# One hundred gathered tokens on one run of partitions, and two table units fetched early

## The reference

```python
def peer(h, w_pq, sub_keys, u_tab, v_tab):
    qr = (h @ w_pq)                                  # 8 heads, two halves of 128
    sc = einsum(qr, sub_keys)                        # 128 scores per half
    s_top, i_top = top_k(sc, 16)                     # 16 of each half
    c_top, c_pos = top_k(all 256 sums of pairs, 16)  # 16 of the 256 pairs
    expert = i0 * 128 + i1                           # 16384 experts
    g = softmax(c_top)
    a = gelu(einsum(u_tab[expert], h), approximate=False)
    return einsum(g * a, v_tab[expert])
x = x + peer(rmsnorm(x, g_ffn), ...)
```

## Time and profile before

| what | value |
|---|---|
| time, median of three runs | 1666.11 us |
| profiled execution, its own time | 1668.66 us |
| its span, first to last instruction | 1666.9 us |
| mean granted TensorE clock | 0.998 |
| busy PE / DVE / ACT / POOL | 1654.3 / 1019.7 / 503.4 / 273.2 us |
| moved by DMA | 569.90 MB |
| first matmul of the u stage at | 511.99 us |
| first matmul of the v stage at | 1101.08 us |

### The profile page before, as it was taken

The page is one execution under the profiler, slowest core; times in us unless marked ns, Lnnn a source line. Parts: engine busy times, 40 slices in busy tenths (PEclk is TensorE's granted clock), DMA queues, the critical chain, the costliest instruction groups (busy, mean ns, idle before and its releaser), DMA issues.

```text
span 1666.9 us, 28850 instructions
## 1 busy us (share of the span) xinstructions
PE 1654.3 (99%) x11438; PEld 1569.3 (94%) x11438; DVE 1019.7 (61%) x1709; ACT 503.4 (30%) x1347; POOL 273.2 (16%) x252
## 2 busy tenths in 40 slices
PE   8999999999999999999999999999999999999999
PEld 6768888888999999999999999999999999999998
DVE  5426695767878999767777767753334333443333
ACT  6547567756551000035444454410000000000000
POOL 1020000000003222312222122121121212211110
PEclk9999999999999999999999999999999999999999
DMA  9764446466648999999999999999999999999996
GB/s 342 240 143 132 140 129 200 139 226 204 227 153 342 421 396 423 417 380 419 404 422 413 422 409 422 422 422 421 421 421 417 417 415 422 422 421 420 421 416 234
DMA packets 107057, 569.90 MB, mean 342 GB/s; under 512 B 11281, under 2 KB 13457, under 8 KB 48209
## 3 DMA queue, kind: packets, MB, share of 16 engines
q1 hardware_dynamic: 56768, 216.22, 35.0%
q0 software_dynamic: 31792, 220.50, 32.7%
q10 hardware_dynamic: 18432, 132.41, 19.3%
HBM read 563.04 MB, written 4.46 MB: 340 GB/s over the span
## 4 chain that ended last, share of the span: by engine, by line
PE 82%; DMA 12%; DVE 3%; issue 1%; ACT 1%; POOL 0%; ACTq 0%; DVEq 0%
PE ps L1586 33%; PE ps L1531 22%; PE ps L1318 5%; PE ps L1323 5%; PE ps L1320 5%; DMA acts<-in_u_rows,sel 5%; DMA late<-in_u_rows,sel 3%; DMA sel<-sel 2%; PE ps L1340 2%; PE ps L1482 2%; PE ps L1478 2%; PE ps L1477 2%; DVE w_lo L821 1%; DMA raw<-in_w_in 1%; PE ps L1548 1%
## 5 line engine op out<-in xcount | busy, mean ns | idle before, releaser
L1145 DVE SCALAR_TENSOR_TENSOR acts<-late,sel,acts 128x2048 f32<-128x2048 f32 x77 | 181.1, 2352 | 247.3 <-DMA late<-in_v_tab,sel 247.0
L1531 PE MATMUL ps<-acts,late 128*128 128x160 f32 x2048 | 287.9, 300 | 0.0
L1531 PE MATMUL ps<-acts,raw 128*128 128x160 f32 x2048 | 287.6, 300 | 0.0
L1586 PE MATMUL ps<-acts,raw 128*128 (+1 forms) x2048 | 283.8, 299 | 0.9 <-DMA raw<-in_v_tab 0.8
L1586 PE MATMUL ps<-acts,late 128*128 (+1 forms) x2048 | 284.2, 299 | 0.0
L1586 PEld LDWEIGHTS ps<-acts,raw 128*128 128x128 f32 x2048 | 279.8, 190 | 1.7 <-issue 1.7
L1531 PEld LDWEIGHTS ps<-acts,late 128*128 128x128 f32 x2048 | 280.5, 190 | 0.1
L1531 PEld LDWEIGHTS ps<-acts,raw 128*128 128x128 f32 x2048 | 280.4, 190 | 0.0
L1586 PEld LDWEIGHTS ps<-acts,late 128*128 128x128 f32 x2048 | 280.1, 190 | 0.1
L821 DVE TENSOR_TENSOR w_lo<-raw,w_hi 128x512 fp32r<-128x512 f32 (+1 forms) x288 | 188.8, 682 | 131.6 <-ACT w_hi L544 129.4
L544 ACT ACTIVATE w_hi<-raw 128x512 fp32r<-128x512 f32 (+1 forms) x288 | 170.3, 622 | 86.9 <-PE ps L1482 41.9
(11 more groups left out here) (224 smaller groups left out, 1526.0 us busy)
## 6 DMA issues: line engine op xcount, KB each, us to landing
raw<-in_w_in SPq DMA_DIRECT2D x72, 512.0 KB, 3.7
raw<-in_u_tab SPq DMA_DIRECT2D x33, 1024.0 KB, 9.6
late<-in_u_tab SPq DMA_DIRECT2D x33, 1024.0 KB, 9.6
raw<-in_v_tab SPq DMA_DIRECT2D x32, 1024.0 KB, 9.9
raw<-in_v_tab ACTq DMA_DIRECT2D x32, 1024.0 KB, 9.9
late<-in_v_tab SPq DMA_DIRECT2D x32, 1024.0 KB, 10.0
late<-in_v_tab ACTq DMA_DIRECT2D x32, 1024.0 KB, 9.9
raw<-in_u_tab ACTq DMA_DIRECT2D x31, 1024.0 KB, 9.5
```

Source lines behind the costliest of these rows:

```text
L1145: V.scalar_tensor_tensor(acc, row[n % NROW], w_sp[:, n - N_OWN:n - N_OWN + 1], acc, ALU.mult, ALU.add).then_inc(row_used, 1)
L1531: ins = mm(ps[:, q, 0:N_DN], ring[q][:, k * P:k * P + P], hF[:, k, :], start=k == 0, stop=k == KD - 1)
L1586: ins = mm(ps[:, pair_bank(k // 2), at:at + N_DN], ring[q][:, k * P:k * P + P], acts[:, ds(i * (4 * N_DN) + q * N_DN, N_DN)], start=first ...
```

## The change

It changes four things.

1. The gathered tokens are 100 instead of 96, and lie on partitions 0 to 99 (owners). Partitions 100 to 124 are the 25 helpers, with four turns of 24 picks; 125 to 127 take no part. The dense tokens are 156. N_OWN becomes 104: gathers 0 to 95 of each table fetch 125 rows, gathers 96 to 103 fetch 100. There are 39 gate groups, the first one chunk later than before.
2. On VectorE the u stage has 104 rows to take by the same chunk. The exception at c % 16 = 15 goes, and on chunks with c % 16 = 0 there are two rows. Copies with a strided part for the helpers become one copy.
3. The first two units of u_tab go into the first 4096 columns of the activation area, issued by SP in the middle of the query weights; units 4 and 5 take the `raw` buffers that units 0 and 1 had.
4. The picked numbers go over in pieces of 8 (two transfers for each of six heads), hidden rows in two more transfers, and there are four transfers back instead of three. The last eight gathers of the v stage have no helpers, so that nothing is sent back after the last row.

```diff
-    SHARE = 4
-    N_SP = P - P // SHARE
+    N_SP, N_HELP, N_SLOT, N_TURN = 100, 25, 4, 24
     N_DN = SEQ - N_SP
-    N_OWN = N_PICK * N_SP // P
-    N_TURN = N_PICK - N_OWN
+    N_OWN = N_PICK - N_TURN
+    N_LENT = N_SLOT * N_TURN
-    FIRST_G = NKEY - 2 * N_GRP
+    FIRST_G = NKEY - 2 * N_GRP - 2
...
-        lenders, helpers = [slice(i, P, SHARE) for i in range(SHARE - 1)], slice(SHARE - 1, P, SHARE)
+        lenders, helpers = [slice(N_HELP * i, N_HELP * i + N_HELP) for i in range(N_SLOT)], slice(N_SP, N_SP + N_HELP)
+        owners, others, workers = slice(0, N_SP), slice(N_SP, P), slice(0, N_SP + N_HELP)
+        first_units = [region(2 * UNIT * i, 2 * UNIT) for i in range(2)]
...
-            with sp.Fori(0, U_PQ // 4) as i:
+            with sp.Fori(0, U_PQ // 8) as i:
                 for j in range(4):
                     load(i * 4 + (B_PQ + j), j, io["w_pq"][ds(i * (4 * P) + j * P, P), :])
+            sp.wait_ge(piece_used, 2 * B_PQ + 2)
+            for j in range(2):
+                sp.dma_start(first_units[j], u_unit(j)).then_inc(first_in[j], 16)
+            with sp.Fori(U_PQ // 8, U_PQ // 4) as i:
+                for j in range(4):
+                    load(i * 4 + (B_PQ + j), j, io["w_pq"][ds(i * (4 * P) + j * P, P), :])
             for j in range(2):
                 sp.wait_ge(lo_done, 2 * (B_U + 2 * j + 1) - 2 * (NRAW - 1))
-                sp.dma_start(ring[j], u_unit(j)).then_inc(unit_in[j], 16)
+                sp.dma_start(ring[j], u_unit(NRING + j)).then_inc(unit_in[j], 16)
...
-                pool.indirect_dma_start(row[n % NROW], None, table, bass.IndirectOffsetOnAxis(ap=idx[:, k:k + 1], axis=0)).then_inc(row_in[n % NROW], 16)
+                parts = workers if k < N_LENT else owners
+                pool.indirect_dma_start(row[n % NROW][parts, :], None, table, bass.IndirectOffsetOnAxis(ap=idx[parts, k:k + 1], axis=0)).then_inc(row_in[n % NROW], 16)
...
-                at = N_OWN + TOPK * (h % 2)
-                pool.dma_start(idx[helpers, TOPK * h:TOPK * h + TOPK], idx[lenders[h // 2], at:at + TOPK]).then_inc(idx_in, 16)
-                pool.wait_ge(idx_in, 16 * (h + 1))
+                for at in range(TOPK * h, TOPK * h + TOPK, 8):
+                    rows, src = lenders[at // N_TURN], N_OWN + at % N_TURN
+                    pool.dma_start(idx[helpers, at:at + 8], idx[rows, src:src + 8]).then_inc(idx_in, 16)
+                pool.wait_ge(idx_in, 32 * (h + 1))
...
-                        V.scalar_tensor_tensor(row[n % NROW], row[n % NROW], 1.0, hs[turn % 2], ALU.mult, ALU.mult,
-                                               accum_out=a_sel[:, n:n + 1]).then_inc(row_used, 1)
+                        V.scalar_tensor_tensor(row[n % NROW][workers, :], row[n % NROW][workers, :], 1.0, hs[turn % 2][workers, :], ALU.mult, ALU.mult,
+                                               accum_out=a_sel[workers, n:n + 1]).then_inc(row_used, 1)
...
             for c in range(FIRST_G + 4, NKEY):
...
-                if rows_done[0] < N_OWN and c % 16 != 15:
-                    next_row()
+                if rows_done[0] < N_OWN:
+                    next_row(2 if c % 16 == 0 else 1)
...
-            for turn in range(3):
+            dve.wait_ge(unit_used, NKEY)
+            for turn in range(N_SLOT):
                 next_row(N_OWN + (turn + 1) * N_TURN - rows_done[0])
...
+            next_row(2 * N_OWN - rows_done[0])
+            dve.wait_ge(row_used, 2 * N_OWN)
+            dve.wait_ge(lent_in, 16 * N_SLOT)
             V.tensor_tensor(acc, acc, lent, ALU.add).then_inc(acc_sum, 1)
```

More of the change, by code:

```diff
@@ L243, in build_block @@
         unit_in = [sem(f"unit_in{i}") for i in range(NRING)]
+        first_in = [sem(f"first_in{i}") for i in range(2)]
         row_in = [sem(f"row_in{i}") for i in range(NROW)]
@@ L415, in _ @@
                 cols = slice(512 * (n // 2), 512 * (n // 2) + 512)
-                rows = helpers if n % 2 else slice(P, SEQ)
+                rows = others if n % 2 else slice(P, SEQ)
                 sp.dma_start(x_rest[n % 2][:, cols], io["x2_scratch"][rows, cols]).then_inc(x2_back, 16)
@@ L420, in _ @@
             sp.wait_ge(acc_sum, 1)
-            for rows in lenders:
-                sp.dma_start(io["out"][rows, :], acc[rows, :]).then_inc(out_sent, 16)
+            sp.dma_start(io["out"][owners, :], acc[owners, :]).then_inc(out_sent, 16)
             for n in range(4):
@@ L512, in _ @@
             gathers(NROW + 24, N_TURN + 2 * NROW)
+            pool.wait_ge(row_used, N_TURN)
+            pool.dma_start(hs[0][helpers, :], hs[0][lenders[2], :]).then_inc(hs_in, 16)
+            gathers(N_TURN + 2 * NROW, N_TURN + 3 * NROW)
             pool.wait_ge(gsp_ready, 1)
@@ L780, in _ @@
                 gelu(c)
-                if c % 2:
+                if c % 2 and c > 1:
                     odd_unit(c + NRING)
@@ L1237, in _ @@
             next_row()
-            gate(0)
-            hots(2)
+            hots(1)
             apply(FIRST_G + 2)
             next_row()
-            gate(1)
-            g = 2
+            gate(0)
+            g = 1
             for c in range(FIRST_G + 4, NKEY):
@@ L1528, in u_chunk @@
                     pe.wait_ge(score_done, 2 * NH)
-                pe.wait_ge(unit_in[q], i * 16 + 16)
+                early_unit = isinstance(i, int) and i == 0 and q < 2
+                if early_unit:
+                    pe.wait_ge(first_in[q], 16)
+                else:
+                    pe.wait_ge(unit_in[q], i * 16 + (16 if q >= 2 else 0))
+                unit = first_units[q] if early_unit else ring[q]
                 for k in range(KD):
-                    ins = mm(ps[:, q, 0:N_DN], ring[q][:, k * P:k * P + P], hF[:, k, :], start=k == 0, stop=k == KD - 1)
+                    ins = mm(ps[:, q, 0:N_DN], unit[:, k * P:k * P + P], hF[:, k, :], start=k == 0, stop=k == KD - 1)
                 ins.then_inc(unit_used, 1)
@@ L1559, in _ @@
                 u_chunk(FG, q)
-                if q >= 2:
-                    gate_group(q - 2, q - 2, True)
-            with pe.Fori(FG + 1, NKEY // 4) as i:
+            gate_group(0, 0, True)
+            for q in range(4):
+                u_chunk(FG + 1, q)
+                if q % 2 == 0:
+                    gate_group(1 + q // 2, 1 - q // 2, q == 0)
+            with pe.Fori(FG + 2, NKEY // 4) as i:
                 for q in range(4):
@@ L1579, in v_chunk @@
             def v_chunk(i, q, first=False, last=False):
-                pe.wait_ge(unit_in[q], i * 16 + (16 * NKEY // NRING + 16))
+                pe.wait_ge(unit_in[q], i * 16 + (16 * NKEY // NRING + (16 if q >= 2 else 0)))
                 for k in range(KD):
```

94 lines of the change are left out of this document (44 added, 50 removed).

## The result

| what | before | after |
|---|---|---|
| median of 4 runs, us | 1666.32 (1665.05 to 1668.33) | 2592.01 (2580.67 to 2602.38) |
| ratio, 95% interval | 1 | 1.5552 (1.5474 to 1.563) |
| profiled span, us | 1666.9 | 2600.6 |
| first matmul of the u stage, us | 512.0 | 508.4 |
| first matmul of the v stage, us | 1101.1 | 1574.9 |

Slower was forecast, by 16 us; it is 926. The u stage begins about when it did (3.6 us earlier). It grew by 477 us (589 to 1066), the rest by 460 (566 to 1026). The bytes grew by 1.5%.

A forecast was written before the change was run, and what follows sets the result against it. DMA was taken as full at 422 GB/s under a TensorE busy nearly throughout. Last gathered row at 1671.4 us plus 11.2 us gave 1682.6, 1682 us on the median; range of all 1653 to 1708.

The forecast's parts named there:

- Item 2: Gather bytes: by the fullest engine, 125 rows cost like 128 and 100 like 112; 14.7 MB more in all.
- Item 6: VectorE and the rest: 37 us of added row work and GpSimd's stops hidden; streams landing in time, 0, bound +3.
- Rival C: Gathers: 125 rows use only five engines, 100 rows ten; slower, range high 1708 leaves out its upper part; chance 0.20.
- Item 1: Dense matmuls of both stages: 156 columns instead of 160 save 3.3 ns per record, 27 us in both.
- TensorE alone: Whole kernel if TensorE sets the end: 28 us earlier, 1638 us.
- Items 3 and 4: u stage, units 52 to 119: 17.3 us later than before; v stage: last gathered row at 1671.4 us, end 1682.6.
- main forecast: Whole kernel, gathers costed by the fullest engine: 1682 us, own range 1672 to 1692, chance 0.43.
- six such stops: GpSimd waiting for passed picked numbers to land: still six stops, hidden while five rows are under way.
- Item 5: Early pair of u units, fetched during the query weights: 0 taken, bounds -5 and +5 us.
- Rival D: Engines can give some 440 GB/s, gathers keep up, TensorE sets the end: 1638 us, half of it 1652; chance 0.17.

The follow-up runs named there:

- e2: The changed kernel with every gather fetching 128 rows, the extra rows unused: 1710.7 us, ratio to before 1.0248.
- e6: The changed kernel with 128-row gathers, but only half of each row fetched and worked on by VectorE: 1640.7 us, ratio 0.9843.
- e3: The kernel before with gathers and VectorE's work on them cut to 125 rows, the last three partitions' work left out: 2526.45 us (one run).
- e9: The changed kernel with 128-row gathers, whole rows fetched, but VectorE works on half of each row: 1705.28 us, ratio 1.0228.
- e7: The kernel before with only the early pair of u units fetched during the query weights: 1668.49 us, ratio 1.0007.
- e1: Small kernel without matmuls: gathers of six row counts, alone and beside SP's streams; median 8 KB packet alone 309 ns with 128 rows, 549 with 125.
- e5: Small kernel loading or gathering different partition sets, each alone; SP's median 8 KB packet 654 ns on partitions 0 to 63, 309 on every second.

## Why the prediction was wrong, and where it held

- *Item 2, bytes: here it failed.* "If the fullest engines are the same ones each time, a gather costs like 128 rows" took the time of a packet (0.312 us, as in every transfer of before) for a constant and asked only how rows are counted. With 128 rows in fact the kernel takes 1710.7; with 125 it takes 2592.0. The packet took 575 ns (GpSimd), 541 (SP) and 523 (ScalarE) instead of 318. By the sum above that is the size of the loss. The range was wide in how many rows an engine has and had no width in how fast it writes them.
- *Item 6, streams "0, bound +3".* The units are read and written as before, but land after 20.4 us instead of 10.0, and TensorE waits 141 us for them between 1800 and 2300 us alone.
- *Rival C.* The warning that counts which aren't multiples of 8 are untested was right, its mechanism was not: the share stayed at 1.02 and the price is not 16/15 or 16/14 but almost 2. Its five engines appear for SP's loads only. The sign that the prediction gave for C (a lower rate with VectorE waiting for rows) did come, but it is the sign of slow packets as well; the share, and the time of a packet, tell the two apart.
- *Item 1, columns: right.* In e2 the v stage starts with one unbroken piece of the chain of waits, 139.93 / 1056 = 132.5 ns a record; 132.6 was forecast.

```profile
1124.70 139.93 PE ps L1603 x1056
```

  With the rows out of the way (e6) the kernel takes 1640.7 us; "TensorE alone" was 1638. In the changed kernel as given, TensorE idled for rows and units, and its granted clock was 0.85 and 0.90 of 2.4 GHz in the first two stretches above, and 0.51, about the level of 1.2 GHz, in the third, where it had nothing to do. The lower clock came with the idle time, and e3 shows it too (0.864 in the mean of the run).
- *Items 3 and 4, how lateness travels: right in kind.* DMA full, rows late, gates late, TensorE late is what the waits show, and in the v stage the last row comes after TensorE's work. In size they can be tried on e2: 218.1 MB of gathers in the same sums give about 1687 us (the main forecast had fewer bytes in its last gathers), and 1710.7 was measured. Of the 23 us missing, about 5 may be VectorE's (e9), which item 6 had as hidden. The sums took 422 GB/s throughout. In e2 the packets come to 410 GB/s from 735 to 1090 us and to 417 in the v stage; put into the same sums, that is an estimated 10 and 7 us. Why the rate is lower there was not tried. One candidate is item 6's "six such stops", taken as hidden: in e2 GpSimd stands 107 us until picked numbers have landed (89 before), and the chain that ended last goes through three of the stops (through two before, 41 us in all):

```profile
785.90 23.80 DMA sel<-sel
...
869.18 23.92 DMA sel<-sel
...
947.13 24.19 DMA sel<-sel
```

  Against it: in e9 GpSimd stands only 52 us there, and the time is nearly e2's. e6 can't decide it, since with shorter queues the stops shrink as well (to 21 us).
- *Item 5, the early pair: right,* 0 taken and 1.0007 measured (e7).
- *Rival D fell,* and so would the main forecast without the slow packets: in e2 the share is 1.00 at 417 GB/s, TensorE idles, the gathers do not keep up, and 1710.7 us is above its 1672 to 1692.

So the change has two faults. The first is the row count, 881 us, mended by one line. The second is that four more tokens are bought with bytes where no DMA time is left; with 128 rows the kernel is still 44 us slower. That bytes are the most of it is shown by e6; 208 gathers move 16.8 MB more than 192, an estimated 40 us at 422 GB/s, and what the other parts of the change add is not separated. No version that does the whole work beat the kernel before.

What the 4-byte packets do (291 in each gather of 125 rows, 16 in one of 128) is open too; with 611 us of engine time they are worth about 38 us of the span.

## What to carry to other kernels

When a change alters the number or the place of the partitions that a transfer covers, its packet time is an unknown, not a constant: measure that shape alone, in a small kernel like e1, or fetch all 128 partitions and leave the extra rows unused. Read the DMA share and the rate together: full share at half the rate means slow packets, a low share means few engines or little work. And where a transfer's queue is slow, look at the other queues, because they pay as well.

## What the hardware showed that was not expected

- An 8 KB packet into SBUF takes 0.31 us with all 128 partitions, and 0.43 to 0.60 us in gathers to 125, 120, 112, 100 or 96 neighbouring ones (e1); in SP's loads 0.61 with 120, 0.45 with 112, 0.54 with 96, 0.65 with 64 and 1.2 with 16. Spread over every second or fourth partition it is 0.31 again (e5).
- Slow packets of one queue make those of the others slow: SP's from 311 to 479 ns beside gathers of 125 rows (e1), 318 to 541 in the whole kernel.
- The same 125 partitions run on 5 engines at 131 GB/s from SP (e5), and on all at 220 GB/s as a gather (e1).
- With 128 rows gathers and streams together reach 423 GB/s (e1), as in the kernel before.
